# Attention with the values as stationary operand for a pair of heads, probabilities scaled on VectorE before they are turned, and six weight low parts in quarter steps on VectorE

## The reference, cut to what matters

```
logits_c = einsum('bgrsd,bgnd->bgrsn', qg, kc) * scale + bias      # 31 compressed keys
o_c = einsum('bgrsn,bgnd->bgrsd', softmax(logits_c), vc)
o_s = einsum('bgrqk,bgqkd->bgrqd', softmax(logits_s), vs)          # selected keys
o_w = einsum('bgrqk,bkgd->bgrqd', softmax(logits_w), vw)           # window
o = g[..., 0:1] * o_c + g[..., 1:2] * o_s + g[..., 2:3] * o_w
y = concatenate([o, b_gate * causal_dwconv(c_gate * x_t)]) @ w_out
```

## Time and profile before

| what | value |
|---|---|
| runs | 1426.13, 1429.01, 1436.88 us, median 1429.01 |
| the profiled execution, its span | 1428.9 us |
| PE busy | 1371.8 us (96%) |
| DVE busy | 698.6 us (49%) |
| ACT busy | 566.9 us (40%) |
| POOL busy | 465.6 us (33%) |
| share of PE in the chain that ended last | 87% |

### The profile page before, as it was taken

One profiled execution on the slowest core, in us unless ns is written; L12 is line 12 of the kernel. 1 busy time (PEld: TensorE's weight loads), 2 busy tenths in 40 slices (PEclk: granted clock), 3 DMA queues, 4 the chain that ended last, 5 costly groups with the idle time before them and its releaser, 6 DMA issues.

```text
span 1428.9 us, 23064 instructions
## 1 busy us (share of the span) xinstructions
PE 1371.8 (96%) x9570; PEld 1131.4 (79%) x9570; DVE 698.6 (49%) x1192; ACT 566.9 (40%) x854; POOL 465.6 (33%) x131
## 2 busy tenths in 40 slices
PE   5999999999999999999999999999999999999998
PEld 3788766776788888888888678888798888888886
DVE  6656686464665333353337435687255454453002
ACT  4435654253342223222125445555364433443112
POOL 0243143024314434434522321121212443344344
PEclk9999999998999999999999999999999999999999
DMA  8763266002222232223214420011222223223311
GB/s 333 249 138 118 71 244 220 3 4 84 94 89 89 92 115 89 89 102 134 89 62 164 167 89 31 30 38 53 75 89 89 89 89 114 93 89 109 112 59 59
DMA packets 24741, 147.93 MB, mean 104 GB/s; under 512 B 2716, under 2 KB 3868, under 8 KB 9024
## 3 DMA queue, kind: packets, MB, share of 16 engines
q1 hardware_dynamic: 21128, 134.21, 26.6%
q10 hardware_dynamic: 3512, 12.26, 3.2%
HBM read 141.74 MB, written 4.72 MB: 103 GB/s over the span
## 4 chain that ended last, share of the span: by engine, by line
PE 87%; DVE 7%; ACT 2%; issue 2%; DMA 1%; POOL 1%; SPq 0%; DVEq 0%; ACTq 0%; POOLq 0%
PE bank L2090 24%; PE bank L2092 23%; PE bank L2091 23%; PE bank L2397 5%; PE bank L1168 2%; DMA raw<-in_weights 1%; PE bank L1159 1%; PE bank L1150 1%; DVE xres L1692 1%; PE bank L2276 1%; DVE act_lo L1689 1%; POOL xres L1330 1%; PE bank L2257 1%; DVE bank L1685 1%; PE bank L1077 1%
## 5 line engine op out<-in xcount | busy, mean ns | idle before, releaser
L1301 POOL TENSOR_TENSOR weight_lo<-raw,weight_hi 128x2048 fp32r<-128x2048 f32 (+2 forms) x90 | 415.1, 4612 | 822.9 <-ACT weight_hi L1349 822.8
L2090 PE MATMUL bank<-act_hi,weight_hi 128*128 128x512 f32 (+1 forms) x1136 | 433.1, 381 | 6.0 <-DVE q L879 1.9
L2092 PE MATMUL bank<-act_hi,weight_lo 128*128 128x512 f32 (+1 forms) x1136 | 422.8, 372 | 0.0
L2091 PE MATMUL bank<-act_lo,weight_hi 128*128 128x512 f32 (+1 forms) x1136 | 422.6, 372 | 0.0
L1349 ACT ACTIVATE weight_hi<-raw 128x2048 fp32r<-128x2048 f32 (+1 forms) x98 | 185.2, 1890 | 393.4 <-PE bank L2092 392.3
L2090 PEld LDWEIGHTS bank<-act_hi,weight_hi 128*128 128x128 f32 x1136 | 214.0, 188 | 48.0 <-issue 8.3
L2092 PEld LDWEIGHTS bank<-act_hi,weight_lo 128*128 128x128 f32 x1136 | 213.7, 188 | 38.6
L2091 PEld LDWEIGHTS bank<-act_lo,weight_hi 128*128 128x128 f32 x1136 | 214.1, 188 | 34.7 <-issue 0.5
L2090 PE MATMUL bank<-weight_hi,hid_hi 128*128 128x512 f32 x352 | 136.9, 389 | 0.0
L2091 PE MATMUL bank<-weight_lo,hid_hi 128*128 128x512 f32 x352 | 136.9, 389 | 0.0
L2092 PE MATMUL bank<-weight_hi,hid_lo 128*128 128x512 f32 x352 | 136.9, 389 | 0.0
(11 more groups left out here) (376 smaller groups left out, 1755.3 us busy)
## 6 DMA issues: line engine op xcount, KB each, us to landing
raw<-in_weights SPq DMA_DIRECT2D x120, 1024.0 KB, 4.8
w<-in_w ACTq DMA_DIRECT2D x2, 2048.0 KB, 12.0
bias_rows<-grow ACTq DMA_DIRECT2D x1, 2560.0 KB
xres<-in_x SPq DMA_DIRECT2D x4, 512.0 KB, 5.8
strip<-bias_rows ACTq DMA_DIRECT2D x1, 2048.0 KB, 9.8
out<-xres SPq DMA_DIRECT2D x3, 512.0 KB, 2.6
row_a<-in_ln_g ACTq DMA_DIRECT2D x2, 512.0 KB, 4.1
row_b<-in_ln_b ACTq DMA_DIRECT2D x2, 512.0 KB, 4.9
```

Of the source, the lines that this page charges most:

```text
L1301: pool.tensor_tensor(wlo[i % SPLIT][:, :size], raw[n % RAW][:, :size], whi[i % SPLIT][:, :size], ALU.subtract).then_inc(lo_ready, 1)
L2090: pe.matmul(o, l[0], r[0], start=first, stop=False)
L2091: pe.matmul(o, l[0], r[1], start=False, stop=False)
L2092: return pe.matmul(o, l[1], r[0], start=False, stop=last)
```

## The change

1. **Order of items.** Heads go in pairs: per tile slc of head 2k, slc of head 2k+1, win of 2k, win of 2k+1.
2. **Scaling first.** VectorE's one-column gate product becomes an operation over all keys: probabilities * (1/sum) * gate, in place, before the turn. TensorE's turn2 waits for `weight_ready` instead of `exp_done`.
3. **Values.** The 64 value columns are stationary and the 128 turned query columns move. Head 2k writes PSUM partitions 0 to 63, head 2k+1 partitions 64 to 127 of bank 4, for all tiles and all three branches, summed in PSUM. Values run once per pair, in every second visit. The compressed branch is turned into `turned_cmp` and joins as two further products in each slc visit. Turned probabilities have four buffers instead of two.
4. **What goes.** `o`, its 64 updates on VectorE, the four cmp value products of 256 columns with their copies, and `turn_o` with its copies. Instead ScalarE and VectorE take high and low part of a pair (128x512) from bank 4, once per pair. Scores and turn2 rotate over banks 5 to 7.
5. **Low parts.** Those of cg1, xt0, xt1, bg0, bg1 and out2_0 move from GpSimd to VectorE, in four steps of 512 columns, at local slots 3, 5, 7 and 9 of the unit before.

```
-BY_VECTOR = [UNIT_AT[name] for name in ("lora0", "k0", ..., "up2_2")]
+BY_VECTOR = [UNIT_AT[name] for name in ("lora0", "k0", ..., "up2_2", "cg1", "xt0", "xt1", "bg0", "bg1", "out2_0")]
...
+ITEMS = [item for k in range(PAIRS) for i in range(TT)
+         for item in ([("cmp", None, i)] if k == 0 else []) + [(br, 2 * k + c, i) for br in ("slc", "win") for c in range(2)]]
...
# plan of banks
+                if st == "values":
+                    b.add((st, item), 4, **(dict(act=1, dve=1) if item in PAIR_END else {}))
...
# VectorE, in a slot behind head_scores
-                    stt(oh, bank(("values", item))[:, 0:HD], weights4[:, item % 4:item % 4 + 1], oh, ALU.mult, ALU.add,
-                        sem=drain(("values", item), "dve"))
+                if step in (6, 10, 14, 18):
+                    low_quarter((*SLOT_UNITS[1:], "out2_0")[n], (step - 6) // 4)
+                if slot - 4 in PAIR_END:
+                    lo_of_pair(PAIR_END.index(slot - 4))
...
-                    ts(weights4[:, item % 4:item % 4 + 1], weights4[:, item % 4:item % 4 + 1],
-                       gate[:, i, 3 * h + part:3 * h + part + 1], sem=S["weight_ready"])
+                    ts(probs, probs, weights4[:, item % 4:item % 4 + 1], gate[:, i, 3 * h + part:3 * h + part + 1],
+                       ALU.mult, ALU.mult, sem=S["weight_ready"])
...
# TensorE
-                    pe.wait_ge(S["exp_done"], item + 1)
+                    pe.wait_ge(S["weight_ready"], PROBS_AT[item] + 1)
...
-                        mm = pe.matmul(b[:, 0:HD], probsT[item % 2][:, tok(j)],
-                                       (vsl if br == "slc" else vwn)[:, j, HD * (h // REP):HD * (h // REP) + HD],
-                                       start=j == 0, stop=j == i)
+                        for c, x in enumerate(pair):
+                            mm = pe.matmul(b[head_of(c), tok(i)], values[:, j, HD * (h // REP):HD * (h // REP) + HD],
+                                           probsT[PROBS_AT[x] % TURNED][:, tok(j)], start=(br, j) == ("slc", 0), stop=(br, j) == ("win", i))
...
-            for t in range(TT):
-                mm = pe.transpose(bank(("turn_o", k))[:, tok(t)], o[:, t, P * k:P * k + P], ident[:])
...
+        def low_quarter(name, part):
+            n = UNIT_AT[name]
+            i, c = SPLIT_AT[n], slice(SEQ * part, SEQ * part + SEQ)
+            if part == 0:
+                dve.wait_ge(lo_ready, i)
+                dve.wait_ge(hi_ready, i + 1)
+            d.step(V.tensor_tensor(wlo[i % SPLIT][:, c], raw[n % RAW][:, c], whi[i % SPLIT][:, c].bitcast(F32),
+                                   ALU.subtract), lo_ready if part == 3 else None)
```

More of the change, by code:

```diff
@@ L135 @@
 RAW, SPLIT = 3, 2
-BY_VECTOR = [UNIT_AT[name] for name in ("lora0", "k0", "out1_3", f"down1_{FT // 2 - 1}", "out2_3", "up2_1", "up1_2", "up2_2")]
+BY_VECTOR = [UNIT_AT[name] for name in ("lora0", "k0", "out1_3", f"down1_{FT // 2 - 1}", "out2_3", "up2_1", "up1_2", "up2_2",
+                                        "cg1", "xt0", "xt1", "bg0", "bg1", "out2_0")]
 HALF = SEQ // 2
@@ L388, in slots_of, with second_of_pair @@
     return range(PER_UNIT * n, min(PER_UNIT * (n + 1), N_SLOTS))
+def second_of_pair(item):
+    return ITEMS[item][0] != "cmp" and ITEMS[item][1] % 2 == 1
 def stages_of(slot):
     return [(st, slot - lag) for st, lag in (("scores", 0), ("turn2", 2), ("values", 3))
-            if 0 <= slot - lag < len(ITEMS)]
+            if 0 <= slot - lag < len(ITEMS) and (st != "values" or second_of_pair(slot - lag))]
 def n_keys(item):
@@ L420, in plan_second @@
             for st, item in stages_of(slot):
-                by_act = st == "turn2" or (st == "values" and ITEMS[item][0] == "cmp")
-                b.add((st, item), **(dict(act=1) if by_act else dict(dve=1)))
-    for k in range(PAIRS):
-        b.add(("turn_o", k), act=1, dve=1)
+                if st == "values":
+                    b.add((st, item), 4, **(dict(act=1, dve=1) if item in PAIR_END else {}))
+                else:
+                    b.add((st, item), **(dict(act=1) if st == "turn2" else dict(dve=1)))
+    b.shared = range(4, 8)
     dense_rows("mix2", "out2_3", act=1)
@@ L564, in build @@
     cgT = here("cgT", [P, 4, SEQ])
+    strip_at = nxt
     strip = here("strip", [P, N_HEADS, SEQ])
-    o = here("o", [P, TT, MIX])
+    out_parts, _ = place("attention_out", [P, N_HEADS, SEQ], F32R, strip_at)
+    out_hi, out_lo = (out_parts[:].rearrange("p (k a) n -> p a k n", a=2)[:, part] for part in range(2))
+    turned_probs = here("turned_probs", [P, 2, SEQ])
+    cmpT = here("turned_cmp", [P, TT, 2 * P])
     blk = here("blk", [P, L_CMP // 2, N_KV * CMP_W])
@@ L759, in second_act @@
                drain(("turn_v", "gates"), "act"))
-        for n, name in enumerate(SLOT_UNITS):
+        for n, unit in enumerate(SLOT_UNITS):
             convert()
@@ L795, in second_act @@
             a.done(act.activation(act_hi[:, 4 + k, :], bgT[:, k, :], ACT.Copy), S["y2_hi"])
-        for k in range(PAIRS):
-            await_full(act, ("turn_o", k))
-            a.done(act.activation(act_hi[:, k, :], bank(("turn_o", k))[:], ACT.Copy), drain(("turn_o", k), "act"))
         act.dma_start(row3[:], src["mix_post"].partition_broadcast(P)).then_inc(load["rows3"], 16)
@@ L920, in convolve, with lo_of_pair @@
                 stt(bgT[:, k, tap:], cgT[:, k, 0:SEQ - tap], col("cmix", 8 - 4 * tap + k), bgT[:, k, tap:], ALU.mult, ALU.add)
+        def lo_of_pair(k):
+            name = ("values", PAIR_END[k])
+            await_drained(dve, name, "act")
+            tt(out_lo[:, k, :], bank(name)[:], out_hi[:, k, :].bitcast(F32), ALU.subtract, sem=drain(name, "dve"))
         def by_group(x):
@@ L1006, in second_dve @@
             lo_of_convolution(k)
-        for k in range(PAIRS):
-            await_full(dve, ("turn_o", k))
-            await_drained(dve, ("turn_o", k), "act")
-            tt(act_lo[:, k, :], bank(("turn_o", k))[:], act_hi[:, k, :].bitcast(F32), ALU.subtract, sem=drain(("turn_o", k), "dve"))
+        lo_of_pair(PAIRS - 1)
         def add_rms(stage, e, t, row, between=()):
```

91 lines of the change are left out of this document (45 added, 46 removed).

## The result

The changed kernel takes 1441.75 us (median of five runs, 1437.95 to 1445.86) beside 1431.95 for the kernel before: ratio 1.0083, 95% interval 1.0060 to 1.0107. It is slower by 10 us by the medians, by 12 by the ratio. The profiled execution has a span of 1440.0 us (before 1428.9).

The account below looks back on a forecast made before the run. TensorE was taken to bound the attention stretch, with VectorE's latency ahead of its next instruction deciding. 1428.9 - 5.1 (values) + 22.0 (late scaling) - 1.7 (GpSimd) - 0.9 (end) = 1443 us; range 1424 to 1454.

Parts of the forecast that it names:

- The likeliest mechanism: In the attention stretch, VectorE's scaling comes late and TensorE's turn waits for it; 1443 us, chance 0.68.
- TensorE's value work: Value products in the attention stretch: 33.9 us before, 21.1 plus 7.7 for switching the array after; 5.1 saved.
- Scaling ahead of the turn: Race from scores through VectorE's scaling to TensorE's turn: late in visits without values, more behind a quarter; 22.0 us added.
- the compressed items: In unit cg0, compressed items already wait 2.9 us for VectorE's scaling; 0.3 more added.
- the carry-over of the convolution: In units xt1 and bg0, convolution steps ahead of head_scores carry part of VectorE's lateness over; 1.5 us each, 3.0 added.
- GpSimd, 1.7 saved: With GpSimd's low parts gone, their clash with a convolution step and TensorE's wait for bank drains go; 1.7 us saved.
- End of the stretch: From last triple to first projection unit: transposes go, bank 4 waits for seven VectorE operations; 5.75 for 6.7, 0.9 saved.
- rival 2: TensorE's clock falls behind idle spells in the attention stretch, three falls costing 9 us more: 1452; chance 0.12.
- The signs named for the clock: A clock under 0.95 over the attention stretch would show the clock-fall rival instead of the main case.
- Rival 1: In the attention stretch VectorE's scaling is in time and TensorE's work decides: 1421 us; chance 0.15.
- Rival 3: The array's halves don't overlap with 128 columns in the value products, 21.1 us more of TensorE: 1461; chance 0.05.

Follow-up runs that it names:

- the longer distance: Changed kernel with the turn three visits behind its scores instead of two, values four instead of three, and a fourth score buffer: 1420.5 us, ratio 0.9943.
- the best place on VectorE: Changed kernel with each quarter step of the low parts moved from ahead of the scaling to behind it, same slot: 1430.9 us, ratio 1.0011.

## Why the prediction was right, step by step

The forecast was 1443, slower by 1%; measured 1441.75, within the range, and slower by 0.83%. The likeliest mechanism was the one that happened. That the two times lie 1 us apart is in part luck: the forecast was 14 us over the kernel before, the profiled spans differ by 11.1 and the medians by 9.8, and the kernel before came out 3 us higher in five runs (1431.95) than in the three that the forecast was set against. The waits were put 4 us too high.

- **TensorE's value work, 5.1 saved:** the records from the first value record of a visit to the next other one sum up to 33.5 us before (taken as 33.9) and 25.8 now in 32 visits (the one that fell on the lower clock counted at its usual 0.59); entering the halves is 0.20 from the last transpose to the first value record where it was 0.11, 3.0 more. 28.8 is the number that was forecast (21.1 + 7.7); 4.7 saved. TensorE's busy time in the stretch shows less of it (156.5 for 156.1), since the lower clock costs 3.4 us more there than before. The Trainium skill, TensorEngine Tiling (Array Packing), Key Properties, has a drain at a change of tiling mode, and the prediction's estimate of it, 3.4 us in all, is too small here: per visit 0.09 us are lost on entering, 0.04 in the first step and 0.11 on the way out (sixteen records take 1.02, eight steps of 0.11 and these two), 0.24 each as forecast. The rows were the better guide.
- **Scaling ahead of the turn, 22.0 added on 2.9:** measured 20.5 in 29 places (about 30 were named) where the forecast had 24.9, so 17.6 were added. Head_scores 0.69, scaling 0.55 and 0.35 (taken as 0.54 and 0.34), the way back 0.14 (taken as 0.15, shown by no row): each price held. A visit with a quarter and one triple was late by 0.9 to 1.1 from unit xt0 on (forecast 1.15; 1.4 once, where VectorE's four blocks stood against TensorE's next scores of one), in cg1 by 0.4 to 0.9, without a quarter by 0.3 to 0.5 (0.42). Cut at the units, the waits are 1.5, 3.9, 4.4, 4.4, 4.7 and 1.7 us, forecast 3.2, 4.3, 4.3, 5.8, 5.8 and 1.4. Mis-sized were the compressed items (1.3 left of 2.9; why, no run tried) and the carry-over of the convolution. Overlooked was the pair's low part, 0.73, which three times stands in the same race; the two times that it met a quarter the waits were 1.73 and 1.72.
- **GpSimd, 1.7 saved:** the second wait of the earlier trace rows is gone, but the cause was wrong. Of its three waits in the kernel before (0.63 at 940.8, 0.60 at 958.4, 0.50 at 963.6) only the last stands behind a convolution step that GpSimd held (1.90 us); the first stands behind one of the usual 0.75. And the kernel before with the quarters alone still has 2.6 us of such waits. As the worth of that part of the change it was wrong by far. A two-scalar operation from SBUF to SBUF is one that GpSimd's low part holds until it ends, and the turn now hangs on it. Without the quarters the change costs 32 us, with them 10. The earlier trace rows showed the mechanism, 2.27 us for a convolution step; I priced it where it stood and didn't ask what the new operation would do beside it.
- **End of the stretch, 0.9 saved:** 5.6 us instead of 6.7, 1.1 saved. That the first product would now wait for the low parts was right, 1.88 us.
- **Clock, rival 2:** it fell in the changed kernel too, to 0.66 over four windows of 5 us. Three lie at the start of the stretch, where the kernel before has its own fall; the fourth is behind the wait of 1.72 at 980.63. So the rival happened once for certain, for 1.7 us, beside the likeliest case and not in its place. It may have happened twice: the fall from 851.6 to 858.5 stands behind the first late turn with a quarter (1.07, at 849.3), and of the other kernels only the one with the quarters one slot later has a fall between 855 and 870. The signs named for the clock held: 0.96 over the stretch, not under 0.95.
- **Sum:** waits 20.5 against 5.5 before (with 0.9 for ScalarE), +15.0; values -4.7; end -1.1; one clock fall +1.7: 10.9, where the profiled spans differ by 11.1. The agreement is looser than it looks: in the profile after the stretch begins 3.9 us earlier (first compressed score at 839.8, before at 843.7) and the clock falls at its start cost 1.7 more. Over all the profiles that begin lies between 836.6 and 846.3 with the falls now ahead of it, now behind, whatever the change, so about 2 us are not accounted for. The stretch ended 11.7 us later where some 15 were named, with TensorE busy 88.3% of it where under 88 was named.

Rival 1's time of 1421 was what the change is worth if VectorE is in time, and the kernel with the longer distance, 1420.5, is that case. The prediction lays the same 1421 to value work done in half the time; by its own numbers that would be 17 saved and not 5.1, so 1409, and 4.7 was measured. Rival 3 is refuted: issued alternately the halves overlap.

## What to carry to other kernels

Before an operation is put between two engines that wait for each other, add up its whole chain against the one visit it has, and count what stands in front of it in program order; here 0.7 us in the wrong place cost as much as the new layout saved, and one more buffer and one visit more of distance gave all of it back. Ask also which engine's long instruction can hold the new one: an operation with time to spare can be held unseen, one on the critical chain can't. Cutting the holder into pieces (1432.0) was worth as much as moving its work to the best place on VectorE (1430.9); on the longer distance the medians give it 5 us more.

## What the runs showed of the hardware

- A GpSimd tensor_tensor on SBUF of 128x2048 (4.5 us) holds a VectorE tensor_scalar from and to SBUF until it ends: 3.65 to 4.37 us instead of 0.35 to 0.55. VectorE's operations that read a bank and one SBUF tensor ran on unhindered inside it (0.56 for 384 columns at 870.72, as everywhere). The Trainium skill, SBUF — State Buffer (Who interferes with whom), says this: GpSimd shares one port pair with VectorE, taken by tensor_scalar in its two-port mode and by operations with two SBUF inputs, and the loser waits for the whole instruction. The trace agrees, for both kinds: the held scaling above, and the compressed operation with two SBUF inputs (2.47), which ended 0.07 after GpSimd's instruction.
- The same work in four pieces held VectorE seldom and never over 1.2 us beyond its usual time.
- Clock falls stand at such waits, though not at every one. All five waits of 3.5 to 4.0 us (no quarters) had one, and the mean granted clock of the stretch was 0.91. Of the two of 1.7 in the changed kernel one had (0.96). With 1.1 at most (the longer distance) the stretch had only the fall at its start, where the kernel before has one too (0.99).
- TensorE starts a record of a free column half ahead of up to three older ones of the busy half. Order within a visit is therefore worth 6 us of the 21 that full overlap saves.
